# Feed-forward's and most of the gated unit's values turned by VectorE's 32x32 blocks and ScalarE's transfers instead of by TensorE

## The reference

```python
def first_block(x, c, positions, w_ada, ...):
    ...
    h = _rmsnorm(x, norm_ffn[l]) * (1.0 + sc_f) + sh_f
    gate, up = jnp.split(h @ w_gate_up[l], 2, axis=-1)        # 2048 -> 2 x 5632
    x = x + gt_f * ((jax.nn.silu(gate) * up) @ w_down[l])     # 5632 -> 2048
    return _rmsnorm(x, final_norm)

def gmlp_mixer(h, w_in, v_gain, w_s, b_s):
    u, v, gate = jnp.split(h @ w_in, 3, axis=-1)              # 2048 -> 3 x 4096
    u = jax.nn.gelu(u)
    v = rmsnorm(jax.nn.gelu(v), v_gain)
    ...
    sv = jnp.einsum('gpq,bnqgc->bnpgc', w_s, vc) + b_s.T[None, None, :, :, None]
    return u * sv.reshape(bsz, seq, D_INNER), gate

def second_block(x, ...):
    ...
    x = x + (y * jax.nn.silu(gate)) @ w_out                   # 4096 -> 2048
    return rmsnorm(x, final_norm)
```

## Time and profile before

| | us |
|---|---|
| median of 3 runs | 2210.5 (2210.04 to 2210.89) |
| the profiled execution | 2210.39 |
| its span, first to last instruction | 2208.8 |
| TensorE busy | 2172.4 |
| VectorE busy | 1503.4 |
| ScalarE busy | 1007.6 |
| mean busy share of the 16 DMA engines | 69% |

### The profile page before, as it was taken

One profiled execution on the slowest core, in us unless ns is written; L12 is line 12 of the kernel. 1 busy time (PEld: TensorE's weight loads), 2 busy tenths in 40 slices (PEclk: granted clock), 3 DMA queues, 4 the chain that ended last, 5 costly groups with the idle time before them and its releaser, 6 DMA issues.

```text
span 2208.8 us, 27097 instructions
## 1 busy us (share of the span) xinstructions
PE 2172.4 (98%) x10488; PEld 1823.5 (83%) x10488; DVE 1503.4 (68%) x1900; ACT 1007.6 (46%) x1284; POOL 24.5 (1%) x26
## 2 busy tenths in 40 slices
PE   7899999999999999999999999999999999999998
PEld 5799988878888888888888888888888888888887
DVE  8989698998897677755454555575556565655556
ACT  5357456433444644443444334464444444444444
POOL 0001000000000000000000000000000000000000
PEclk8999999999999999999999999999999999999999
DMA  9975568997798588866555565566665666565663
GB/s 404 420 280 164 185 225 275 306 315 266 266 355 286 189 295 297 286 217 193 191 186 190 192 195 189 183 202 198 191 197 182 193 194 195 187 191 189 193 192 127
DMA packets 241552, 507.01 MB, mean 230 GB/s; under 512 B 19304, under 2 KB 34960, under 8 KB 235920
## 3 DMA queue, kind: packets, MB, share of 16 engines
q1 hardware_dynamic: 241424, 505.28, 68.6%
HBM read 503.10 MB, written 2.12 MB: 229 GB/s over the span
## 4 chain that ended last, share of the span: by engine, by line
PE 84%; DVE 8%; DMA 5%; ACT 1%; issue 1%; SPq 0%; DVEq 0%; POOL 0%; ACTq 0%
PE bank L1254 25%; PE bank L1256 25%; PE bank L1255 25%; DVE WL L2072 3%; DVE RAW L2059 2%; DMA A<-in_w_cd_dram 2%; PE bank L1445 1%; PE bank L1186 1%; PE bank L1261 1%; PE bank L1263 1%; PE bank L1262 1%; DMA RAW<-in_w_ada_dram 1%; DMA RAW<-in_w_cd_dram 1%; DMA RAW<-in_w_cq_dram 1%; ACT WH L1522 1%
## 5 line engine op out<-in xcount | busy, mean ns | idle before, releaser
L2072 DVE TENSOR_TENSOR WL<-RAW,WH 128x1024 fp32r<-128x1024 f32 x706 | 860.4, 1223 | 566.7 <-ACT WH L1522 558.4
L1522 ACT CAST WH<-RAW 128x1024 fp32r<-128x1024 f32 x706 | 738.5, 1049 | 837.4 <-PE bank L1256 702.8
L1254 PE MATMUL bank<-WH,HTh 128*128 128x512 f32 x1922 | 757.9, 394 | 3.1 <-DVE WL L2072 3.1
L1256 PE MATMUL bank<-WH,HTl 128*128 128x512 f32 x1922 | 749.0, 390 | 0.0
L1255 PE MATMUL bank<-WL,HTh 128*128 128x512 f32 x1922 | 748.3, 389 | 0.0
L1254 PEld LDWEIGHTS bank<-WH,HTh 128*128 128x128 f32 x1922 | 361.0, 188 | 78.2 <-DVE WL L2072 5.0
L1256 PEld LDWEIGHTS bank<-WH,HTl 128*128 128x128 f32 x1922 | 360.7, 188 | 76.1
L1255 PEld LDWEIGHTS bank<-WL,HTh 128*128 128x128 f32 x1922 | 361.1, 188 | 72.7
L1254 PE MATMUL bank<-WH,R2h 128*128 128x512 f32 x408 | 160.2, 393 | 0.3 <-DVE WL L2072 0.3
L1256 PE MATMUL bank<-WH,R2l 128*128 128x512 f32 x408 | 158.9, 390 | 0.0
L1255 PE MATMUL bank<-WL,R2h 128*128 128x512 f32 x408 | 158.8, 389 | 0.0
(11 more groups left out here) (299 smaller groups left out, 1816.5 us busy)
## 6 DMA issues: line engine op xcount, KB each, us to landing
RAW<-in_a_w_in_dram SPq DMA_DIRECT2D x192, 512.0 KB, 3.8
RAW<-in_w_gate_up_dram SPq DMA_DIRECT2D x176, 512.0 KB, 4.5
RAW<-in_w_ada_dram SPq DMA_DIRECT2D x128, 512.0 KB, 5.5
RAW<-in_w_in_dram SPq DMA_DIRECT2D x112, 512.0 KB, 5.0
RAW<-in_w_down_dram SPq DMA_DIRECT2D x88, 512.0 KB, 4.3
RAW<-in_a_w_out_dram SPq DMA_DIRECT2D x64, 512.0 KB, 3.7
A<-in_w_ada_dram SPq DMA_DIRECT2D x17, 1024.0 KB, 14.0
RAW<-in_w_o_dram SPq DMA_DIRECT2D x32, 512.0 KB, 5.7
```

The lines of the kernel that those rows point to most:

```text
L1254: e.matmul(o, ah[:, s], hi[:, k, :], start=first, stop=False)
L1256: i = e.matmul(o, al[:, s], hi[:, k, :], start=False, stop=last)
L1522: e.copy(hi, rv).then_inc(S["hi"], 1)
L2072: e.tensor_tensor(lo, rv, hi.bitcast(F32), ALU.subtract).then_inc(S["lo"], 1)
```

## The change

The 11 chunks `ff` (`FF_TURNED`) and the first 6 of the 8 chunks `y` (`Y_TURNED`) are turned without TensorE. In slot 2 VectorE transposes the whole chunk in 32x32 blocks from AN or YN to the new place TQ (`sx_t`). In slot 3 ScalarE issues sixteen DMAs from TQ to TD (`sx_s`), each for one group of 32 source partitions and one group of 32 target partitions, 8 runs of 32 words for each partition: 32 KB in 256 runs of 128 bytes, within SBUF. In slot 6 ScalarE waits for all sixteen and copies TD to the high part, 128x1024 at once, and VectorE subtracts for the low part (`sx_h`). The chunks `mix`, y 6 and y 7 stay with TensorE; the bank numbers and waits of those get counters of their own. TQ and TD lie where FN2 lies, so FN2 is now loaded by a step of its own, `load_fn2`, after the low part of chunk y 5.

```diff
--- before.py
+++ after.py
@@ -278,6 +278,7 @@
+        self.TQ, self.TD = ar(88, 1024), ar(92, 1024)
@@ -327,6 +328,7 @@
+FF_TURNED, Y_TURNED = range(11), range(6)
@@ -352,6 +354,7 @@
+        self.sx_of, self.hl_t_of, self.hl_turned = {}, {}, 0
@@ -928,10 +931,25 @@
+        if (kind == "ff" and c in FF_TURNED) or (kind == "y" and c in Y_TURNED):
+            m = self.sx_of[kind, c] = len(self.sx_of) + 1
+            self.put("sx_t", kind, c, m)
+            yield
+            self.put("sx_s", m)
+            for _ in range(3):
+                yield
+            self.hl_n += 2
+            self.put("sx_h", kind, c, m, self.hl_n)
+            self.hl_of[kind, c, 0] = self.hl_of[kind, c, 1] = self.hl_end[m] = self.hl_n
+            self.have |= {("hl", kind, c, 0), ("hl", kind, c, 1)}
+            if (kind, c) == ("y", Y_TURNED[-1]):
+                self.put("load_fn2", m)
+            return
         for g in range(2):
             self.hl_n += 1
-            self.put("hl", kind, c, g, self.hl_n)
-            self.hl_of[(kind, c, g)] = self.hl_n
+            self.hl_turned += 1
+            self.put("hl", kind, c, g, self.hl_n, self.hl_turned)
+            self.hl_of[(kind, c, g)], self.hl_t_of[kind, c, g] = self.hl_n, self.hl_turned
@@ -941,7 +959,7 @@
-                self.put("gate_t", name, c, 4 + (self.hl_n + 2) % 4)
+                self.put("gate_t", name, c, 4 + (self.hl_turned + 2) % 4)
@@ -1117,6 +1135,12 @@
+
+
+def tokens_read(sch, name, c):
+    if (name, c) in sch.sx_of:
+        return ("sx_t", sch.sx_of[name, c])
+    return ("hl_t", sch.hl_t_of[name, c, 1])
...
@@ -1372,11 +1396,11 @@
-            n = 4 + (num - 1) % 4
+            n = 4 + (nt - 1) % 4
             take(n)
             four(bank[n], [src[:, q % 2, (2 * g + q // 2) * P:(2 * g + q // 2 + 1) * P] for q in range(4)]
                  ).then_inc(S["hl_t"], 1)
-            held[n] = [("hl_lo", num)]
+            held[n] = [("hl_lo", args[3])]
@@ -1740,15 +1764,33 @@
-            name, c, g, num = args
-            bk = bank[4 + (num - 1) % 4].rearrange("p (k t) -> p k t", t=T)
-            W.wait_ge("hl_t", num)
+            name, c, g, num, nt = args
+            bk = bank[4 + (nt - 1) % 4].rearrange("p (k t) -> p k t", t=T)
+            W.wait_ge("hl_t", nt)
             hi, _, k = hl_target(L, name, c, g)
             W.wait_ge("half", hl_free(sch, name, c))
             if name == "mix":
                 e.activation(hi[:, k:k + 2, :], bk, ACT.Copy, scale=0.5).then_inc(S["hl_hi"], 1)
             else:
                 e.copy(hi[:, k:k + 2, :], bk).then_inc(S["hl_hi"], 1)
+
+        elif kind == "sx_s":
+            m, = args
+            W.wait_ge("sx_t", m)
+            if m > 1:
+                W.wait_ge("hl_lo", sch.hl_end[m - 1])
+            for tq in range(4):
+                for cq in range(4):
+                    src = L.TQ[32 * tq:32 * tq + 32, :].rearrange("p (n c t) -> p n c t", c=4, t=32)[:, :, cq, :]
+                    dst = L.TD[32 * cq:32 * cq + 32, :].rearrange("p (n q t) -> p n q t", q=4, t=32)[:, :, tq, :]
+                    e.dma_start(dst, src).then_inc(S["sx_in"], 16)
+
+        elif kind == "sx_h":
+            name, c, m, _ = args
+            hi, _, k = hl_target(L, name, c, 0)
+            W.wait_ge("sx_in", 256 * m)
+            W.wait_ge("half", hl_free(sch, name, c))
+            e.copy(hi[:, k:k + 4, :], L.TD.rearrange("p (k t) -> p k t", t=T)).then_inc(S["hl_hi"], 2)
@@ -1920,7 +1962,7 @@
-        return ("half", job_end(sch, "down", (1, 3))) if place == EXTRA_T[0] else ("hl_t", sch.hl_of["ff", 10, 1])
+        return ("half", job_end(sch, "down", (1, 3))) if place == EXTRA_T[0] else tokens_read(sch, "ff", 10)
@@ -2342,7 +2384,8 @@
-            W.wait_ge("hl_t", sch.hl_of["mix", c - 2, 1] if c > 1 else 0)
+            if c > 1:
+                W.wait_ge(*tokens_read(sch, "mix", c - 2))
@@ -2365,6 +2408,24 @@
+
+        elif kind == "sx_t":
+            name, c, m = args
+            W.wait_ge("an" if name == "ff" else "yn", 2 * c + 2)
+            if m > 1:
+                W.wait_ge("sx_in", 256 * (m - 1))
+            src = L.AN if name == "ff" else L.YN
+            e.transpose(L.TQ.rearrange("p (k b n) -> p k b n", k=4, b=2), src.rearrange("p b (k n) -> p k b n", k=4)
+                        ).then_inc(S["sx_t"], 1)
+
+        elif kind == "sx_h":
+            name, c, m, num = args
+            hi, lo, k = hl_target(L, name, c, 0)
+            W.wait_ge("sx_in", 256 * m)
+            W.wait_ge("hl_hi", num)
+            W.wait_ge("half", hl_free(sch, name, c))
+            e.tensor_tensor(lo[:, k:k + 4, :], L.TD.rearrange("p (k t) -> p k t", t=T), hi[:, k:k + 4, :].bitcast(F32),
+                            ALU.subtract).then_inc(S["hl_lo"], 2)
@@ -2468,7 +2529,8 @@
-            W.wait_ge("hl_t", sch.hl_of["ff", c - 1, 1] if c else 0)
+            if c:
+                W.wait_ge(*tokens_read(sch, "ff", c - 1))
@@ -2527,7 +2589,8 @@
-            W.wait_ge("hl_t", sch.hl_of["y", g - 1, 1] if g else 0)
+            if g:
+                W.wait_ge(*tokens_read(sch, "y", g - 1))
@@ -2761,6 +2824,9 @@
+
+        elif kind == "load_fn2":
+            W.wait_ge("hl_lo", sch.hl_end[args[0]])
```

More of the change, by code:

```diff
@@ L1366, in pe_program @@
         elif kind == "hl":
-            name, c, g, num = args
+            name, c, g, _, nt = args
             src = L.MX[c % 2] if name == "mix" else L.AN if name == "ff" else L.YN
```

## The result

The changed kernel takes 2306.2 us (median of 4, 2303.14 to 2310.97) against 2210.6: 4.33% slower, a ratio of 1.0433 (95% interval 1.0421 to 1.0445). The prediction was 2214, with a range of 2199 to 2242. The profiled execution took 2306.46 us, its span is 96.0 us longer than in the earlier trace rows.

The account below looks back on a forecast made before the run. TensorE was taken to bound the kernel, helpers following it. Terms -16.5 + 5.0 + 4.5 + 8.3 + 2.0 = +3.3 us on the profiled 2210.39 gave 2214 us, range 2199 to 2242.

Parts of the forecast that it names:

- The path and the saving: TensorE bounds the kernel; each of 17 chunks turned without it saves 0.97 us, 16.5 us in all.
- VectorE's work and the copies: Block transpose 1.24 us, copy 1.05 and subtraction 1.22 us a chunk on VectorE and ScalarE, counted at nothing.
- The lead: ScalarE's splits run ahead of TensorE, so the sixteen issues may take 7.1 us before TensorE stands.
- P: Start of the job after a turned chunk; times counted from it in halves of a weight tile, 2.72 us each.
- The length of an issue: Sixteen DMA issues in a row on ScalarE: 0.37 us, then 0.48 for each further one, 7.6 us a chunk.
- The ends (6.5 and 9.4 us): Range for a chunk's row of sixteen issues on ScalarE, at 0.41 and 0.60 us for each of 15.
- The stall: TensorE waits before half 6 after a chunk: 0.5 us for ten feed-forward chunks, 0.75 for six of the gated unit.
- chunk 10: Read by the very next job, down (2, 0), from its fifth half, so without cover: TensorE stands 8.3 us.
- long issues: Rival: ScalarE's issues exceed 0.48 us, each 0.01 more costing 2.6 us in all; 2234 at 0.56, 2258 at 0.65; chance 0.22.
- my 2 us for the four full chunks: First four feed-forward chunks, DMA share already 0.8: moves may land late, between 0 and 13 us, taken as 2.
- slower: Outcome of the whole change beyond the 2206.1 to 2214.9 us counted as the same; chance 0.48.

Follow-up runs that it names:

- 17 turns without gaps (10 and 7 chunks): Changed kernel with ScalarE issuing four DMAs in each of slots 3 to 6, copy in slot 8, chunk 10 on TensorE, y 6 turned: 2194.99 us, ratio 0.9928.
- the short rows from HBM: Changed kernel with DMA sources by chunk in turn (HBM, SBUF over 128 partitions, as changed): 2273.39 us; HBM rows of 7.4 to 7.6 us left 0.61 to 0.75 us gaps.

## Why the prediction was wrong, step by step

**The path and the saving held.** 17 x 0.97 = 16.5 us was forecast; 17 turns without gaps (10 and 7 chunks) give 16.8.

**VectorE's work and the copies cost nothing**, as said: 1.24 us for the transpose, 1.04 and 1.22 for the halves, and no gap from them without the moves.

```profile
L2418 DVE STREAM_TRANSPOSE A<-A 128x1024 f32<-128x1024 f32 x17 | 21.1, 1240 | 0.0
...
L1793 ACT CAST aTh<-A 128x1024 fp32r<-128x1024 f32 x11 | 11.4, 1041 | 0.0
...
L2427 DVE TENSOR_TENSOR aTl<-A,aTh 128x1024 fp32r<-128x1024 f32 x11 | 13.4, 1221 | 0.0
```

**The lead held.** The issues may take 7.1 us. In chunk 9 they begin at P + 6.6 (forecast P + 6.75) and the next split at 1383.76 = P + 17.95; 2.4 us later TensorE can go on, at 1386.21 = P + 20.4, in place of P + 16.3. The gap between starts is 4.1 us longer than it should be, and 11.3 - 7.1 = 4.2. Behind the short rows from HBM the stall was the forecast one. The count of halves was sound.

**The length of an issue failed**, and it is the term that I called the first to look at. I took 0.37 + 15 x 0.48 = 7.6 us from SyncE's loads; a row takes 10.5 us at 0.66 an issue and up to 12.0 with a long one in it, 10.9 on average. The step that failed is the choice of the nearest row: I explained the longer issues of the earlier trace rows by backlog and took the shorter. All my rows were loads from HBM, where for transfers of this size 0.48 is right; a copy out of SBUF has another price, and I had no row of one. The ends (6.5 and 9.4 us) were built from the same loads and so too narrow. The stall was forecast as 10 x 0.5 + 6 x 0.75 = 9.5 us and is 59.6; for chunk 10 8.3, and it is 11.0.

**The clock was missing from the sum.** I had a row for its level and none for what a gap does to it, and put each us of idle TensorE at one us. The sum with measured terms: -16.5 + 59.6 + 11.0 = 54.1. An idle time counts from the end of a matmul of 0.39 us though the next would start after 0.23, which is 17 x 0.16 = 2.7 more. The span is 96.0 longer, so 39.2 are left. From the other side: TensorE works through 77 us at the low clock, and there the loss is 1 - 0.23/0.43 = 0.47, 36 us. The two agree to 3 us; the first matmuls behind a gap, which start 0.34 and 0.26 us apart before the clock has fallen in chunk 9, are part of the rest. The clock is thus about two fifths of the 96 us, and most of the reason why my own rival "long issues", at 0.65 us an issue, gave 2258 and not 2306: its 2.6 us for 0.01 held for the stall alone.

The Trainium skill (TensorE: Matmul & The Clock Gate, HAM oscillation) says that a matmul loop cut by waits can fall back to the low clock behind each one and pay in every turn, and prices it as half the time spent low. By that all 96 us at the low clock cost 48 and the 77 in which TensorE works 38, both estimates; the trace has 36 to 39, so it agrees for the time that is worked through and not for the whole. I had not weighed it, because I expected gaps of 0.5 us, and at that length the runs show no fall. But I also forecast one of 8.3 us at chunk 10, where it belonged in the sum: in the version without the moves that gap was 3.8 us and cost 1.7 more by the clock.

**DMA.** In the changed kernel nothing waits for the moves to land. From the first issue to the last landing it is 12 to 13 us, so my 2 us for the four full chunks were not there. Packets of 128 B in place of 1 KB cost little: landing takes 2.4 us at the median with either. The Trainium skill (DMA: Bandwidth & Descriptors, Why small descriptors are slow (HBM only)) has short packets within SBUF as free of the penalty that they have with HBM; the trace agrees. The same page says, in Issuing engines are not separate DMA queues, that issuing from several engines saves only the sequencer's time, usually small beside the DMA itself. One issue is (0.63 us against 2.4 to land), but a row of sixteen holds the splits behind it: moving the row off ScalarE, or breaking it up, was worth 93 and 97 us.

**The chances** had 0.22 on long issues and nothing beyond 0.65 us with a clock behind it; slower had 0.48 and was right, but only in its sign.

## What to carry to other kernels

A DMA issue cost its engine's queue 0.37 to 0.66 us here, now and then 1.2 to 2.1, so count a row of them like compute: compare its length with the lead of whatever stands behind it, and break the row at each piece of work that has a due time. Price a gap on TensorE at its length plus the stretch at half clock that it can bring: here gaps of 3.5 us and more nearly always did, at 1.4 to 3 us each, and those up to 1.8 us never. A sum that stops at idle time can miss half as much again. Where no row of the trace shows the operation with the same source and destination, its range has to be wide, and the forecast is to be tried at its upper end too.

## What the runs showed of the hardware that I had not expected

- With 32 KB a DMA, an issue in a row takes 0.44 to 0.47 us with its source in HBM and 0.61 to 0.63 with it in SBUF, whether ScalarE or SyncE makes the latter, for 32 or 128 partitions and for 128 B or 1 KB packets. Some rows (5 of 17 in the changed kernel) have one issue of 1.2 to 2.1 us, each with a fetch of instructions by the DMA engines at that moment.
- Gaps up to 1.8 us, start to start, left the clock alone; at 2.2 us each of three brought half clock, at 3.35, 3.77 and 4.15 one didn't; in the changed kernel all 17 did (3.55 us and more). What decides in between was not settled, nor why the low stretch is 3.4 us in one place and 6.8 in another.
- The clock's fall doesn't wait for TensorE to start again: in 14 of the 17 gaps it came while TensorE stood, so part of the low stretch costs nothing.
- The moves, of 128 B packets within SBUF, landed 1.9 to 5.7 us after their own issue, 2.4 at the median, beside the weights' transfers (106 to 286 GB/s in all in the windows around chunk 9).
